# A two-block sequence model on one core: the first block's mixing products computed from split operands, and the modulation sums in another order

## What is computed

```python
def hybrid_layer(...):                       # first block, layers l = 0, 1
    h = rmsnorm(x, norm_mix)
    (a_x, a_b, a_c, d_q, d_k, d_v, i_q, i_k, i_w,
     g_q, g_f, g_i, g_g, m_q, gate_logits) = split_cols(h @ w_in)
    y_a = a_b * causal_conv3(a_c * a_x, conv_w)
    y_b = dsa_attention(...)     # index scores, top-64 per row, softmax attention, 8 heads
    y_c = hgrn2 recurrence in chunks of 64, 4 heads, from g_q, g_f, g_i, gated by g_g
    y_m = attention of m_q over 256 memory tokens (keys, values: mem_n @ mem_w_kv)
    gates = sigmoid(gate_logits)             # 4 branches x 1024
    merged = sum(gates[n] * (branch[n] @ w_lift[n]) for n in range(4))
    x = x + merged @ w_out
    return x + swiglu feed-forward, width 2816
# second block, layers 2 and 3 of the feed-forward count:
#   sh, sc, g, ... = silu(c) @ mod_w[i] + mod_b[i]        (modulation, a row of 6 x 1024)
#   for layer 0 of it also silu(c_ctx) @ mod_w[0], of which two of the six parts are used
```

## Time and profile before

| | us |
|---|---|
| median of three runs | 2472.51 |
| profiled execution, its own time | 2467.38 |
| its span | 2465.6 |
| PE busy | 2293.0 (93%) |
| DVE busy | 1259.1 (51%) |
| ACT busy | 659.3 (27%) |

### The profile page before, as it was taken

One profiled execution on the slowest core, in us unless ns is written; L12 is line 12 of the kernel. 1 busy time (PEld: TensorE's weight loads), 2 busy tenths in 40 slices (PEclk: granted clock), 3 DMA queues, 4 the chain that ended last, 5 costly groups with the idle time before them and its releaser, 6 DMA issues.

```text
span 2465.6 us, 33483 instructions
## 1 busy us (share of the span) xinstructions
PE 2293.0 (93%) x14158; PEld 1902.1 (77%) x14158; DVE 1259.1 (51%) x2224; ACT 659.3 (27%) x882; POOL 57.5 (2%) x79
## 2 busy tenths in 40 slices
PE   6999989999989999799999998898899989989997
PEld 5858768699978587686999687877489967546996
DVE  3341346688733413444888366546355553634544
ACT  1113320043301133200444153321143411003442
POOL 0000000001000000000000000000010000000000
PEclk9999989999999999899999998999899999999999
DMA  6433326678644332267785321110265542203551
GB/s 212 150 111 115 116 81 226 209 252 279 211 135 149 120 119 103 86 222 249 244 281 201 92 73 65 36 36 2 63 188 187 171 141 79 97 0 115 186 186 68
DMA packets 207754, 348.68 MB, mean 141 GB/s; under 512 B 20643, under 2 KB 111562, under 8 KB 207221
## 3 DMA queue, kind: packets, MB, share of 16 engines
q1 hardware_dynamic: 192704, 291.15, 34.9%
q0 software_dynamic: 14624, 55.31, 6.8%
q10 hardware_dynamic: 276, 0.08, 0.0%
HBM read 345.48 MB, written 1.05 MB: 141 GB/s over the span
## 4 chain that ended last, share of the span: by engine, by line
PE 75%; DVE 17%; ACT 5%; issue 2%; DMA 1%; SPq 0%; DVEq 0%; ACTq 0%
PE psum L375 53%; PE psum L716 20%; DVE ring_low L1042 4%; DVE A L1506 3%; DVE G L1169 2%; ACT high_weights L1035 1%; DVE wide_room L1169 1%; ACT A L819 1%; PE psum L434 1%; DVE A L1169 1%; DVE tmp L1169 1%; DMA ring<-in_w_in_dram 1%; PE psum L420 1%; PE psum L694 0%; DVE xn L1469 0%
## 5 line engine op out<-in xcount | busy, mean ns | idle before, releaser
L375 PE MATMUL psum<-hT,ring 128*128 128x256 f32 (+1 forms) x3472 | 689.4, 360 | 16.3 <-DVE G L1169 7.1
L375 PEld LDWEIGHTS psum<-hT,ring 128*128 128x128 f32 x3472 | 602.5, 196 | 92.7 <-DVE G L1169 7.3
L1042 DVE TENSOR_TENSOR ring_low<-ring,high_weights 128x2048 fp32r<-128x2048 f32 x124 | 284.2, 2292 | 169.6 <-ACT high_weights L1035 167.6
L716 PE MATMUL psum<-high_rows,high_weights 128*128 128x256 f32 x1280 | 364.1, 284 | 4.8 <-DVE ring_low L1042 4.8
L716 PE MATMUL psum<-high_rows,ring_low 128*128 128x256 f32 x1280 | 362.4, 283 | 0.0
L716 PEld LDWEIGHTS psum<-high_rows,high_weights 128*128 128x128 f32 x1280 | 242.5, 189 | 7.0 <-issue 6.3
L716 PEld LDWEIGHTS psum<-high_rows,ring_low 128*128 128x128 f32 x1280 | 244.7, 191 | 0.0
L1035 ACT ACTIVATE high_weights<-ring 128x2048 fp32r<-128x2048 f32 x124 | 237.8, 1917 | 3.9
L1506 DVE SCALAR_TENSOR_TENSOR A<-A,silu_c 128x256 f32<-128x256 f32 x392 | 190.1, 485 | 14.0
L716 PE MATMUL psum<-yT_low,high_weights 128*128 128x256 f32 x640 | 181.2, 283 | 0.0
L716 PE MATMUL psum<-x2T_low,high_weights 128*128 128x256 f32 x640 | 180.1, 281 | 0.0
(11 more groups left out here) (409 smaller groups left out, 2485.5 us busy)
## 6 DMA issues: line engine op xcount, KB each, us to landing
ring<-in_w_in_dram SPq DMA_DIRECT2D x36, 2048.0 KB, 7.7
ring<-in_ffn_w_dram SPq DMA_DIRECT2D x66, 1024.0 KB, 5.3
A<-in_mod_w_dram POOLq DMA_DIRECT2D x48, 1024.0 KB, 7.7
ring<-in_ffn_w_up_dram SPq DMA_DIRECT2D x44, 1024.0 KB, 5.3
ring<-in_ffn_w_down_dram SPq DMA_DIRECT2D x22, 1024.0 KB, 6.9
ring<-in_w_lift_dram SPq DMA_DIRECT2D x16, 1024.0 KB, 8.4
ring<-in_ab_w_in_dram SPq DMA_DIRECT2D x7, 2048.0 KB, 7.9
ring<-in_hy_w_in_dram SPq DMA_DIRECT2D x6, 2048.0 KB, 8.0
```

What stands on the lines that cost most here:

```text
L375: return pe.eng.matmul(out, lhsT, rhs, start=(k == 0), stop=(k == n - 1))
L716: ins = pe.eng.matmul(out, lhs[a], rhs[b], start=first and n == 0, stop=last and n == 2)
L1042: v.eng.tensor_tensor(low, whole, high.bitcast(F32), ALU.subtract).then_inc(*v.mark(f"w_lo/{l}.{i}"))
```

## The change

1. **Split products in mixing.** 17 panels per layer (`a_c`, `a_b`, `i_q`, `d_q`, `g_f`, `g_q`, `g_i`, `g_g`, `m_q` and the eight gate halves) are multiplied as three fp32r products. Each panel is cut in 4 parts of 128x1024, 68 parts per layer, numbered in the order of use. ScalarE makes the high part in a room, VectorE the low part in `ring_low`. The rooms are taken in turn: five for parts 0 to 39, three for parts 40 to 50 (gate half 0.1 to 1.1), six from part 51. A part's room is free once TensorE has finished its last user (`half/...`). `a_x`, `small`, `lift`, `out` and the memory's products stay in float32.
2. **Where the parts are made.** `prepared(l, form, h)` on ScalarE and `lows(l, form, h)` on VectorE make all parts, in order, up to the first whose room's last user is not before part h of panel `form`, or whose panel can't be there yet. Such calls are put at some 20 places of both programs.
3. `split_tokens` takes the banks of both token halves before its first product.
4. `small` comes second in the plan and on TensorE; the constants and the memory's norm on VectorE come after the first low parts. The token rows h are split too (four ScalarE copies, four VectorE subtractions per layer).
5. **Modulation.** `MOD_ORDER` puts the one-row parts 8 to 15 with layer 0's merge units and the two-row parts 0 to 7 in its feed-forward, one in each of steps 0 to 7; layer 1's feed-forward has two and one in turn (16), layer 2's one in each of steps 0 to 7. The first of a step now stands between `act` and `act_low`; TensorE's sum stands before `down`.
6. The scan of the recurrence is done in two halves; `mergedT` is the room of `hT`; some rooms move.

```diff
+MODULATIONS = {0: (8, (1,) * 8 + (0,) * 3), 1: (24, (2, 1) * 5 + (1,)), 2: (40, (1,) * 8 + (0,) * 3)}
+MIX_MODULATIONS = (0, 16)
+MOD_ORDER = tuple(range(8, 16)) + tuple(range(8)) + tuple(range(16, 48))
 def mod_rows(i):
-    return 2 if i < 8 else 1
+    return 2 if MOD_ORDER[i] < 8 else 1
...
+    for i in range(PARTS_IN_ALL):
+        if i < first_part["gate{}.0.1"]:
+            rooms_ = ("a", "b", 10, 4, 5)
+        elif i < FIRST_LATE:
+            rooms_ = ("a", "b", 10)
+        else:
+            rooms_ = ("a", "b", 10, 2, 8, 9)
...
+    def parts_open(l, form, h):
+        end = first_part[form] + h if form else 0
...
+            if late or part_user[i][0] >= end or any(place_of(z) >= at for z in top["loaded_after"][split_part(l, i)[0]]):
+                return i
...
+        def split_unit(form, l, u, label):
+            b = take(label)
+            for c in range(2):
+                i = first_part[form] + 2 * u + c
+                wh, wl, used = split_ready(l, i)          # waits for mix_lo/{l}.{i}
...
+                for k in range(KD):
+                    ins = product(b[:, c * SEQ:(c + 1) * SEQ], (wh[:, k, :], wl[:, k, :]), (rows_high[:, k, :], rows_low[:, k, :]),
+                                  k == 0, k == KD - 1)
...
+        def split_tokens(name, l):
+            labels = [f"{name}_ready/{l}.{t}" for t in range(MT)]
+            b = [take(label) for label in labels]
...
+        def split_high(l, i):
+            a.wait_ge(*reached("panel " + name))
+            if before_ >= 0:
+                a.wait_ge(*reached(f"half/{l}.{before_}"))
...
+            copy(high, whole, f"mix_hi/{l}.{i}")
...
         def sigmoid_of(l, n, q):
+            prepared(l, f"gate{{}}.{n}.{q // 2}", 2 * (q % 2) + 1)
...
+            prepared(l, "gate{}.0.1", 0)
             rsqrt(f"mk_rs0/{l}", A2[:, 0:1024], A3[:, 0:1024], [f"mk_ms/{l}"])
             sigmoid_of(l, 0, 2)
...
+            while lows_done[l] < parts_open(l, form, h):
+                v.wait_ge(*reached(f"mix_hi/{l}.{i}"))
+                tt(low, whole, high.bitcast(F32), ALU.subtract, f"mix_lo/{l}.{i}")
...
         def merge(l, n, q):
+            lows(l, f"gate{{}}.{n}.{q // 2}", 2 * (q % 2) + 1)
...
+            lows(l, "gate{}.0.1", 0)
             v.wait_ge(*reached(f"pT/{l}.1.3"))
...
+            for i in modulation_steps(l, j - 1) if j else []:
+                modulation_done(v, i)
+            steps = modulation_steps(l, j)
+            for i in steps[:1]:
+                modulation_scaled(v, i)
             v.wait_ge(*reached(f"act_hi/{l}.{j}"))
...
             low_part(v, l, PIECES.index((True, j, 0)))
-            for i in modulation_steps(l, j - 1) if j else []:
-                modulation_done(v, i)
-            for i in modulation_steps(l, j):
+            for i in steps[1:]:
                 modulation_scaled(v, i)
```

More of the change, by code:

```diff
@@ L193, in panel_plan @@
         pair = lambda n, half: [f"gate{l}.{n}.{half}", f"lift{l}.{n}.{half}"]
-        plan += [f"{n}{l}" for n in ("a_x", "a_c", "a_b", "small", "i_q", "d_q", "g_f", "g_q", "g_i", "g_g", "m_q")]
+        plan += [f"{n}{l}" for n in ("a_x", "small", "a_c", "a_b", "i_q", "d_q", "g_f", "g_q", "g_i", "g_g", "m_q")]
         plan += pair(0, 0) + [f"m_k{l}", f"m_v{l}"] + pair(0, 1)
@@ L230, in modulation_steps @@
 def modulation_steps(l, j):
-    if l >= DEPTH or j >= FFN_STEPS:
+    if l not in MODULATIONS or j >= FFN_STEPS:
         return []
-    two = 16 - FFN_STEPS
-    return [24 * l + 8 + i for i in ([2 * j, 2 * j + 1] if j < two else [two + j])]
+    first, slots = MODULATIONS[l]
+    at = lambda j_: first + sum(slots[:j_])
+    return list(range(at(j), at(j + 1)))
+MODULATIONS = {0: (8, (1,) * 8 + (0,) * 3), 1: (24, (2, 1) * 5 + (1,)), 2: (40, (1,) * 8 + (0,) * 3)}
+MIX_MODULATIONS = (0, 16)
+MOD_ORDER = tuple(range(8, 16)) + tuple(range(8)) + tuple(range(16, 48))
 FILTER_STEPS = (4, 6, 8)
@@ L468, in merge_unit @@
             half, u = q // 2, q % 2
[L469 to L476, removed]
+            split_unit(f"gate{{}}.{n}.{half}", l, u, f"gate_ready/{l}.{n}.{q}")
             w, used = panel(f"lift{l}.{n}.{half}")
@@ L546, in tensor @@
                     ins.then_inc(*pe.mark(f"q_sum_ready/{l}"))
-                    transposed("g_f", l, None)
-                    transposed("g_q", l, None)
-            tokens("g_i", l, None)
-            tokens("g_g", l, None)
+                    split_transposed("g_f", l)
+                    split_transposed("g_q", l)
+            split_tokens("g_i", l)
+            split_tokens("g_g", l)
             for t in range(MT):
@@ L1294, in dve_program @@
             tt(kT[:, :], kT[:, :], rot_t[:, 1, :], ALU.mult, f"kT/{l}")
+            e.memset(attT[:, :, :], 0.0).then_inc(*v.mark())
+            v.wait_ge(*v.own())
             for t in range(MT):
                 W = P * (t + 1)
+                lows(l, ("d_q{}", "g_q{}")[t], 3)
                 v.wait_ge(*reached(f"relu/{l}.{t}"))
@@ L1384, in dve_program @@
             cum = A3[:, 1024:2048]
[L1385 to L1386 removed]
+            for half in range(2):
+                cc = slice(half * HALF, (half + 1) * HALF)
+                e.tensor_tensor_scan(cum[:, cc], consts["chunk_scan"], A3[:, cc], 0.0, ALU.mult, ALU.add).then_inc(*v.mark())
+                v.wait_ge(*v.own())
             c3 = cum.rearrange("p (c t) -> p c t", t=CHUNK)
@@ L1491, in ffn_dve @@
             modulation_done(v, i)
+        if l == 2:
+            top["gains"](range(3, 5))
     def modulation_scaled(v, i):
@@ L2500, in convolve @@
                     f"{label}/{n}" if c else None)
-        gains(range(3, 5))
+        gains([2])
         for t in range(MT):
```

243 lines of the change are left out of this document (191 added, 52 removed).

## The result

The changed kernel took **2412.6 us** (median of 4 runs, 2409.94 to 2413.57), the kernel before 2472.51: a ratio of 0.9756, 95% interval 0.9744 to 0.9768. The forecast was 2415. The time is right within 2.4 us; three of the terms behind it are not, and they cancel in part, which is luck. The profiled execution took 2413.57 us with a span of 2411.8, 53.8 us less than the span before. (That execution of before lay 5.1 us under its median, this one 1.0 over its own; the offset that I kept constant was chance, and is the larger part of the difference between 53.8 and the medians' 59.9.)

What follows compares the result with a forecast made beforehand. Mixing was taken as bound by TensorE's float32 products. Terms -83.6 + 31.4 - 4.9 = -57 us took the profiled 2467.4 to 2410, with the 5.1 us offset to the median 2415 us; range 2380 to 2450 us.

Steps and rivals of the forecast that it cites:

- the offset that I kept constant: Whole kernel: the median lies 5.1 us above the profiled execution, before and after, turning 2410 into 2415 us.
- Price of the products, -83.6: Mixing: three split products replace each float32 one on TensorE, saving 41.8 us per layer, 83.6 us in both.
- New waits, +31.4: Mixing: waits the new parts bring, 1.2 at `g_i` plus 14.5 us per layer, 31.4 us in both.
- part 43 ... Wait 6.3 us: Unit (0,3) of mixing: TensorE waits 6.3 us for part 43's late low part, plus 1.7 us of clock.
- The second `attT`: Mixing: TensorE's wait before it grows from 1.83 to some 2.7 us, with nothing charged for the clock.
- `split_tokens`, +1.2 per layer: At `g_i` in mixing: taking both banks makes TensorE's 4.65 us wait 1.2 us longer.
- Feed-forward, -4.9: Feed-forwards 0 and 1: modulation between `act` and `act_low` removes TensorE's waits of 2.0 and 2.9 us.
- What was late after that is nothing: Feed-forward steps: after the reorder `act_low` and `down`'s low part come before TensorE wants them, so no wait.
- Layer 2's sums, +3.3: Feed-forward 2: modulation sums moved out of layer 0's mixing add 3.3 us here.
- The second block, 0: Stretch of the second block up to feed-forward 2: no change in length, 0 us.
- Rival A: Mixing: no new waits, since both helper engines are half idle; 2384 us, chance 0.20.

Runs made afterwards that it cites:

- `ffn_order_undone`: Changed kernel with the old order of modulation work on VectorE and TensorE in the feed-forwards, only the new slots kept; 2422.67 us.
- `all_five`: Changed kernel plus five edits: keys' sums first, part 43 earlier, `attT` and merge (1,2) earlier, feed-forward 1's last step free, last `down` panels split early; 2368.67 us.
- `no_lows`: Changed kernel without VectorE's low parts in mixing, TensorE using the high part in their place; 2392.61 us.
- `att_bank`: Changed kernel with the second `attT` and the merge of (1,2) put before low parts 50 to 54 on VectorE; 2399.14 us.

## Why the prediction was right, and where it was not

- **Price of the products, -83.6: right.** 5.73 us a unit against 5.70, and +77.8 us when they are taken back, the rest being cover.
- **New waits, +31.4: mis-sized, and one in the wrong place.** With -41.8 for the products, and -3.3 for modulation that left layer 0, the stages leave 45.1 - 26.7 = 18.4 and 41.8 - 24.1 = 17.7 us, **36.1** for both. The step that failed is "part 43 ... Wait 6.3 us". I had counted the rooms of the parts and not the banks: the sums that VectorE reads late hold a bank that TensorE needs next. Before unit (0,2) it cost 4.60 us and 3.7 of clock, 8.3, where I had 6.3 and 1.7, 8.0. That the sums agree is luck; they are different waits. The named costs of layer 0 come to 8.3 here, 4.7 at the second `attT`, 1.5 at `ks`, 1.4 at the copies of `kstok`, 1.2 at `g_i` and 0.5 at the first `attT`: 17.6 of the 18.4.
- **The second `attT`: mis-sized.** Wait right in kind (3.6 us, I had some 2.7), clock charged at nothing. The clock cost 2.9 us in layer 0, and taking the low parts away from it brought 5.2 us per layer, more than twice the wait that went. I had set against the rule of the Trainium skill (TensorE: Matmul & The Clock Gate, Part 1: The HAM clock gate) that an idling array is throttled, and kept the row. The rule agrees with the 0.57 behind this wait. The row was too thin a reason: it is from layer 0, and the same wait in layer 1 of the same trace has 0.79 behind it and cost 1.5 us.
- **`split_tokens`, +1.2 per layer: the wait is right, the price is not.** Undone, it brings nothing.
- **Feed-forward, -4.9: wrong in both halves.** Feed-forward 0 gained 9.3, not 2.0. I had looked at the middle of the steps alone, by the earlier trace rows; in the kernel before, a modulation in the last step also held up the hand-over to the next layer by 5.9 us (rows below). VectorE's `modulation_done` waited for TensorE's sum, which stood behind all `down` products, and the residual stood behind it. A slot table with an empty tail takes that away: with it and the old order (`ffn_order_undone`) nothing stands in the way of the hand-over (0.5 us for `hT`, as in the changed kernel). But by itself it brings only 2.2 us (212.7 to 210.5), since eight steps with two rows then cost TensorE 0.85 us in six of them; the new order removes those. The 9.3 us need both. Feed-forward 1 gained 0.1, not 2.9: the new order saves its waits in the middle and makes one of 4.84 us in the last step, where no `up` products cover the modulation. "What was late after that is nothing" holds for steps 0 to 9 and fails in step 10.

```profile
702.28 1.97 PE L434 MATMUL psum<-const_sb,xn 128*128 128x128 f32 x8 [5.94 <-DVE xn L1139]
```

```profile
696.45 0.16 DVE L1517 TENSOR_TENSOR mod<-psum,columns 128x2 f32<-128x2 f32 x1 [6.17 <-PE psum L694]
696.64 1.41 DVE L1169 TENSOR_TENSOR x<-x,psum 128x512 f32<-128x512 f32 x2
```

- **Layer 2's sums, +3.3: right** (+3.9). **The second block, 0:** +2.0 to feed-forward 2, within what the same stretch varied between runs.

In the sum: waits 4.7 us worse than forecast, feed-forwards 0 and 1 4.3 us better (9.2 against 4.9), everything behind them 2.8 us worse; the span fell by 53.8 us against 57. Rival A (2384) comes nearest to the kernel without VectorE's low parts in the way, 2392.6 measured. With the low parts made, but in another order, mixing alone got 19.8 us shorter (`all_five`), against 22.8 without them (`no_lows`): it was not a matter of whether the engine has time but of what stands in front of what.

## What to carry to other kernels

When work is given to an engine that is half idle, walk through its program order twice: once for the data that others wait for, once for the PSUM banks and buffers that its reads set free. Look at the last step of every loop by itself, since what hides a piece of work in the middle is not there at the end. And price a wait on TensorE at its length and then at its length plus the slow products behind it: here those added 3.7 us to one of 4.6 and 2.9 to one of 3.6. Look at every place with a wait of that length, not at one, before charging nothing.

## What the runs showed of the hardware

- TensorE's clock behind a wait does not follow from the wait's length. Behind the second `attT`, 1.83 us left it at 1.00 in layer 0 of the kernel before and at 0.79 in layer 1, 1.68 us at 1.00 in both layers of `att_bank`; behind one wait of 1.95 us it was 0.58 in one run and 1.00 in another. Behind 3.6 us it was 0.57 over the next 8 us, and behind 4.6 us the slow products lost 3.7 us. Cutting the 3.6 us wait to 1.7 gained 5.2 us per layer.
- A wait shortened by 1.2 us, from 5.87 to 4.65, gained nothing: the clock stayed low for 5.7 us of products instead of 4.0, in the two traces compared. Of these two waits, both followed by a low clock, the shorter was no cheaper. I had not expected that.
- Three split products cost 3 x 0.117 to 0.12 us for 128x256, in mixing as in the feed-forward; one float32 product 0.216 to 0.22 per half of its two records.
